# Stream weights one place later, a gate product that waits, and a decay by TensorE and ScalarE, in a fused mLSTM and latent attention step

## The reference, cut to what matters

```python
s = jnp.einsum('bhtd,bhsd->bhts', q, k) * w_intra
num = w_inter[..., None] * jnp.einsum('bhvk,bhtk->bhtv', C, q) + jnp.einsum('bhts,bhsv->bhtv', s, v)
...
decay = jnp.exp(b_last + m - m_new)
C_new = decay[..., None, None] * C + jnp.einsum('bhsv,bhsk->bhvk', v * w_upd[..., None], k)
n_new = decay[..., None] * n + jnp.einsum('bhs,bhsk->bhk', w_upd, k)
...
y = (hn.astype(x.dtype) + skip * xc) * jax.nn.silu(z)
```

## Time and profile before

| | |
|---|---|
| median of 3 runs | 992.86 us (992.49 to 997.19) |
| profiled execution | 993.93 us, its span 992.0 us |
| PE busy | 970.4 us (98% of the span) |
| DVE busy | 558.6 us (56%) |
| POOL busy | 480.8 us (48%) |
| ACT busy | 413.8 us (42%) |
| HBM traffic over the span | 165 GB/s in the mean, 330 to 416 GB/s in the slices of the heads |

### The profile page before, as it was taken

One profiled execution on the slowest core, in us unless ns is written; L12 is line 12 of the kernel. 1 busy time (PEld: TensorE's weight loads), 2 busy tenths in 40 slices (PEclk: granted clock), 3 DMA queues, 4 the chain that ended last, 5 costly groups with the idle time before them and its releaser, 6 DMA issues.

```text
span 992.0 us, 11792 instructions
## 1 busy us (share of the span) xinstructions
PE 970.4 (98%) x4220; PEld 622.8 (63%) x4220; DVE 558.6 (56%) x1126; ACT 413.8 (42%) x810; POOL 480.8 (48%) x434
## 2 busy tenths in 40 slices
PE   7999999999989999999999999999999999999998
PEld 5776776767645353443535777777766666657885
DVE  5875572745667677976856522246734444456445
ACT  3576876766674734537231000011222423243221
POOL 1585885977525847668364262233630303133330
PEclk9999999999989999999999999999999999999999
DMA  7215134343286998999898422203210111203202
GB/s 281 91 60 211 61 111 162 112 147 127 85 332 230 376 416 330 394 370 361 336 341 334 154 85 85 84 23 109 97 66 32 57 43 45 110 16 134 87 24 106
DMA packets 45721, 164.37 MB, mean 166 GB/s; under 512 B 4884, under 2 KB 8344, under 8 KB 36704
## 3 DMA queue, kind: packets, MB, share of 16 engines
q1 hardware_dynamic: 45664, 163.63, 44.7%
HBM read 106.33 MB, written 57.28 MB: 165 GB/s over the span
## 4 chain that ended last, share of the span: by engine, by line
PE 66%; DVE 4%; ACT 1%; issue 1%; DMA 0%; SPq 0%; ACTq 0%; DVEq 0%
PE work_a L1188 5%; PE bank L1314 5%; PE work_b L1611 5%; PE work_a L834 4%; PE work_a L1164 4%; PE work_b L1485 3%; PE bank L1155 3%; PE work_b L834 3%; PE work_b L1140 3%; PE work_b L1314 3%; PE bank L1572 2%; PE work_a L1597 2%; PE bank L1206 2%; PE work_a L1557 1%; PE work_b L1473 1%; PE bank L1731 1%
## 5 line engine op out<-in xcount | busy, mean ns | idle before, releaser
L3057 POOL TENSOR_TENSOR arena<-arena 128x640 f32<-128x640 f32 x96 | 138.7, 1462 | 36.7 <-ACT arena L1772 34.2
L2560 DVE SCALAR_TENSOR_TENSOR arena<-arena,bank 128x512 f32<-128x512 f32 x128 | 87.0, 742 | 38.1 <-PE bank L1155 38.1
L3260 POOL COPY arena<-arena 32x640 f32<-32x640 f32 x20 | 19.2, 959 | 121.3 <-ACT arena L2097 115.0
L956 PE MATMUL work_a<-arena,ring 128*128 128x320 f32 x224 | 64.9, 433 | 0.0
L956 PE MATMUL work_a<-arena 128*128 128x320 f32 x224 | 64.9, 433 | 0.0
L956 PE MATMUL work_b<-arena 128*128 128x320 f32 x224 | 62.7, 433 | 0.0
L1188 PE MATMUL work_a<-arena 128*128 128x512 f32 x128 | 61.2, 606 | 0.0
L956 PEld LDWEIGHTS work_b<-arena 128*128 128x128 f32 x224 | 42.7, 191 | 17.6
L956 PEld LDWEIGHTS work_a<-arena 128*128 128x128 f32 x224 | 42.7, 190 | 17.6
L956 PEld LDWEIGHTS work_a<-arena,ring 128*128 128x128 f32 x224 | 42.4, 190 | 17.2
L1826 ACT ACTIVATE bank<-arena 128x320 f32<-128x320 f32 x96 | 47.0, 522 | 3.5
(11 more groups left out here) (432 smaller groups left out, 2144.7 us busy)
## 6 DMA issues: line engine op xcount, KB each, us to landing
ring<-in_stream SPq DMA_DIRECT2D x66, 512.0 KB, 3.4
arena<-in_c SPq DMA_DIRECT2D x32, 1024.0 KB, 8.1
out_s_c<-arena SPq DMA_DIRECT2D x32, 1024.0 KB, 5.9
arena<-in_keys SPq DMA_DIRECT2D x8, 664.0 KB, 4.1
z_scratch<-arena SPq DMA_DIRECT2D x16, 320.0 KB, 3.1
v_scratch<-arena SPq DMA_DIRECT2D x20, 256.0 KB, 2.3
k_scratch<-arena SPq DMA_DIRECT2D x4, 1280.0 KB, 5.3
arena<-k_scratch SPq DMA_DIRECT2D x4, 1280.0 KB, 9.3
```

The source lines that it names most:

```text
L956: last = mm(quarter[q], weights[:, k, :], tokens_of[:, k, :], start=fresh and k == 0, stop=k == KH - 1, skip_group_check=True)
L2560: op = v.scalar_tensor_tensor(ct[s % CS][:, g, :], ct[s % CS][:, g, :], decb[:, h, b:b + 1], bank[g][:, :], ALU.mult, ALU.add)
L3057: op = g.tensor_tensor(dst, dst, parts[(adds[0] - adds[1]) % len(parts)], ALU.add)
```

## The change

It has three parts.

`stream_weights(h + 1)` leaves the place ahead of `weight_args(h + 1)` and stands behind `weighted_scores(h + 1, 1)`, for each of the 3 changes of head. Its wait on `m_rows` goes to `weight_args`. Head 0's own instance ahead of the loop stays.

POOL's `gated(h, prompt)` gets one more wait in heads 0 to 2: for all 5 of `weight_args(h + 1)`.

`first_n` goes. In its place `decsel` is made 4 times as wide (4x128, once for each q), a second matmul with one output column turns it into a decay for each of the 128 rows, DVE's copy takes that column along (33 columns for 32), and ACT multiplies `n_rows` by it, in head 0 between `normalise(0, 3)` and `next_keys(0, 0)`. The host sends `p_rows` as zeros, so the load L702 has 260 columns for 164. The wait of `new_n(0)` is now on ACT's instruction.

```diff
-        decsel = shaped(kwsum[:, 0, 0:HEADS * STREAMS], (HEADS, STREAMS))
-        decb = take(HEADS, STREAMS)
+        decsel = shaped(kwsum[:, 0, 0:KH * GROUP], (KH, HEADS, STREAMS))
+        decb_rows = take(GROUP + 1)
+        decb, dec_rows = shaped(decb_rows[:, 0:GROUP], (HEADS, STREAMS)), decb_rows[:, GROUP:GROUP + 1]
...
-            op = mm(bank[0][:, DEC_AT:DEC_AT + HEADS * STREAMS], ones_f[0:HEADS, :],
-                                decsel[0:HEADS].rearrange("p a b -> p (a b)"), start=True, stop=True)
+            mm(bank[0][:, DEC_AT:DEC_AT + GROUP], ones_f[0:HEADS, :], decsel[0:HEADS, 0].rearrange("p a b -> p (a b)"),
+               start=True, stop=True)
+            op = mm(bank[0][:, DEC_AT + GROUP:DEC_AT + GROUP + 1], decsel[0:HEADS].rearrange("p q a b -> p (q a b)"),
+                    ones_f[0:HEADS, 0:1], start=True, stop=True)
...
                 normalise(h, 3)
+                if h == 0:
+                    act.wait_ge(base_in, 16 * 4)
+                    nc.scalar.activation(n_rows, n_rows, ACT.Copy, scale=dec_rows).then_inc(n_decayed, 1)
                 next_keys(h, 0)
...
             def stream_weights(h):
-                if h:
-                    dve.wait_ge(m_rows, 16 * (h + 2))
...
             def weight_args(h):
                 if h:
+                    dve.wait_ge(m_rows, 16 * (h + 2))
...
-            def first_n():
-                dve.wait_ge(base_in, 16 * 4)
-                selected = p_rows[:, 0:GROUP]
-                op = v.tensor_tensor(selected, decb.rearrange("p a b -> p (a b)"), own_dec, ALU.mult)
-                op.then_inc(dve_own, c.up(dve_own))
-                dve.wait_ge(dve_own, c.all(dve_own))
-                v.reduce_sum(dec_rows, selected, AX_X).then_inc(dve_own, c.up(dve_own))
-                dve.wait_ge(dve_own, c.all(dve_own))
-                v.tensor_scalar(n_rows, n_rows, dec_rows, None, ALU.mult).then_inc(dve_own, c.up(dve_own))
-                v.memset(p_rows, 0.0).then_inc(dve_own, c.up(dve_own))
-                dve.wait_ge(dve_own, c.all(dve_own))
...
                 if h == 0:
-                    first_n()
+                    dve.wait_ge(n_decayed, N_DECAYED)
...
-                    head_front(h + 1)
+                    weight_args(h + 1)
...
                     weighted_scores(h + 1, 1)
+                    stream_weights(h + 1)
                     stream_queries(h + 1)
...
+                if more:
+                    pool.wait_ge(dmax_ready, TT * (h + 2))
                 gated(h, slice(0, SEQ), 1)
```

More of the change, by code:

```diff
@@ L270, in program @@
          pv_mm, norm_done, turn_mm, turn_out, pc_mm, pc_out, y_added, weights_summed, prod_mm, prod_kept, prod_sum, y_mixed, pool_mixed, basis_x_ready, inverse_in_sbuf, inverse_in_psum) = (sem(n) for n in names)
+        n_decayed, N_DECAYED = inverse_in_psum, 2
         x_in = [sem(f"x_in{n}") for n in range(4)]
@@ L367, in program @@
         assert top[0] <= c_at, top[0]
[L369 to L372, removed]
+        n_input = rstd[:, HALF:HALF + 2 * P + HEADS]
+        both_rows, p_rows, n_rows = (n_input[:, a:b] for a, b in ((0, 2 * P), (0, P), (P, 2 * P)))
+        own_row = n_input[:, 2 * P:2 * P + HEADS]
         gate_rows, b_row, a2 = arena[:, 0:HALF], rstd[:], msel
@@ L2465, in _ @@
             onehot = rowc[R, R_ONEH:R_ONEH + HEADS]
-            op = v.tensor_tensor(decsel[R], dec_row[R, 0:STREAMS].unsqueeze(1).to_broadcast([HEADS, HEADS, STREAMS]),
-                                            onehot.unsqueeze(2).to_broadcast([HEADS, HEADS, STREAMS]), ALU.mult)
+            op = v.tensor_tensor(decsel[R], dec_row[R, 0:STREAMS].unsqueeze(1).unsqueeze(1).to_broadcast([HEADS, KH, HEADS, STREAMS]),
+                                            onehot.unsqueeze(1).unsqueeze(3).to_broadcast([HEADS, KH, HEADS, STREAMS]), ALU.mult)
             op.then_inc(sel_ready, c.up(sel_ready))
             dve.wait_ge(G.bfill[0], c.next(G.bfill[0]))
-            op = v.tensor_copy(decb.rearrange("p a b -> p (a b)"), bank[0][:, DEC_AT:DEC_AT + HEADS * STREAMS])
+            op = v.tensor_copy(decb_rows, bank[0][:, DEC_AT:DEC_AT + GROUP + 1])
             op.then_inc(cols_ready, c.up(cols_ready))
@@ L2590, in add_skip @@
                                            h_t[:, q, part], ALU.mult, ALU.add).then_inc(raised, c.up(raised))
-            def head_front(h):
-                stream_weights(h)
-                weight_args(h)
             dve.wait_ge(bc_out, 1)
@@ L3456, in _lay_out @@
     n0 = at("state_mlstm_n")[0][..., within].reshape(STREAMS, HEADS, KH, P).transpose(3, 1, 2, 0)
-    row = np.arange(P) % GROUP
-    n_rows = np.concatenate([n0.transpose(2, 1, 3, 0).reshape(P, P), row[:, None] // STREAMS == np.arange(HEADS)[None, :],
-                             row[:, None] == np.arange(GROUP)[None, :]], axis=1).astype(f)
+    row_head = np.arange(P) % GROUP // STREAMS
+    n_rows = np.concatenate([np.zeros((P, P), f), n0.transpose(2, 1, 3, 0).reshape(P, P),
+                             row_head[:, None] == np.arange(HEADS)[None, :]], axis=1).astype(f)
     half = ROPE // 2
```

## The result

| | before | changed |
|---|---|---|
| median, 7 runs each, side by side | 995.75 us | 989.09 us |
| ratio changed / before | | 0.9942 (95%: 0.9923 to 0.9962) |
| profiled execution: time, span | 993.93, 992.0 us | 990.84, 988.9 us |

The ratio is 5.8 us, between 3.8 and 7.7.

A forecast was written before the change was run, and what follows sets the result against it. PE, busy 98%, was taken as the bound, so only its waits and slow spells pay. Back 3.87 + 2 x 1.20 = 6.27, lost 0.3 + 3 x 0.2 = 0.9: 5.4 us less, 987.5 us, range 986.4 to 990.6.

The forecast's parts named there:

- `first_n` off DVE: Change from head 0 to 1: PE's 2.4 us wait and the clock dip behind it go, 3.87 us back.
- next in line: Head 0 to 1, what could hold PE next: POOL's sums (2.8 us spare), step 7's C tile (0.4), DVE's list (2.9).
- The decay on ACT: Head 0: one ACT instruction of 0.4 us, load wait 0 to 0.3, swallowed by idle time; PE loses nothing.
- The wider selection and the second matmul: Ahead of the heads, on PE's path: 0.2 us for the matmul and 0.1 for the selection, 0.3 lost once.
- The stream weights moved, the product held: Later two changes of head: first weighted scores begin 1.4 us earlier, 1.20 us back each; 0.2 lost per change.
- The term of 0.2 us: Each of three changes of head: loss from the queue behind `stream_weights` and a collision with POOL, ends 0 and 0.55.
- The product later: POOL's gate product ends 2 us later; `inverse_root` and the next load of z behind it lose nothing.
- The wait in `weight_args`: Head 0: the wait for the prompt's C store, reached 4 us earlier, may hold DVE where it waits for PE anyway.
- The moved collision: Rival: POOL's small instructions and sum hit the stream work, up to 1.2 us per head change; 990.5 us, chance 0.18.
- The clock-or-DMA case: Rival, head 0: a late C tile or clock dip leaves only 1.8 of 3.87 us back; 989.6 us, chance 0.13.
- The slower one: Rival, head 0: ACT waits for the `n_rows` load, deciding at about 15 us landing; 995.5 us, chance 0.03.
- The signs: Right: PE's waits gone, clock 1.00, head changes 16.5 to 17 us. Wrong: C-tile wait, over 0.6 us lost ahead of heads.

The follow-up runs named there:

- e1: Kernel before with the stream weights moved and the gate product held, `first_n` left on DVE: ratio 0.9988 to the kernel before.
- e2: Changed kernel with both moves undone, leaving only the decay by a matmul and ACT: ratio 0.9980 to the kernel before.
- e3: Changed kernel without POOL's new wait, so the gate product is not held: ratio 0.9985 to the kernel before.
- e4: Changed kernel with `stream_weights` back ahead of the weight arguments and POOL's wait kept: ratio 0.9932 to the kernel before.
- e5: Changed kernel with the stream queries one place later, behind tile 2's weighted scores: ratio 0.9953 to the kernel before.
- e9: Changed kernel with the load of `n_rows` issued one step later: ratio 1.0036 to the kernel before, span 995.5 us.
- e8: Changed kernel, unedited, run again on another chip with a second profile: ratio 0.9956 to the kernel before, span 987.9 us.

## Why the prediction was right, point by point

**The time.** Forecast 987.5 us from a median of 992.86, 0.54% less, in a range of 986.4 to 990.6. Measured were 989.09 and ratios of 0.58% and 0.44% less. The later runs showed that 992.86 was a low median for the kernel before (others 993.4 to 995.75), so the ratio is the better measure, and 5.4 us lies inside both its intervals (3.8 to 7.7 and 2.9 to 5.8). That the medians came so near is partly luck. The spans of the two profiles are only 3.1 and 4.1 us shorter: the heads gave 4.3 and 5.0 us, where the forecast had 5.7, and 1.3 and 1.2 were lost ahead of them, where it had 0.3.

**What bounds it.** Right: PE's two waits were `first_n` (e1, e2) and the gate product (e3, e4), each shown by itself.

**`first_n` off DVE, 3.87 us.** The wait and the dip are gone, as said. The term was too large by the wait for the C tile: A of head 0 came to 6.85 and 6.08, not 5.93. That was the second of the "next in line", with 0.4 us to spare by the prediction. It became a wait of 0.85 us, because the tile landed 12.7 us behind its issue, not 11.4; issue and need had both moved by the same 1.3 us. The rival had this at a cost of 2 us with the dip; it came at 0.9 at most, and without one.

**The decay on ACT: nothing.** Right. The instruction took 0.42 us, and ACT still sat idle 0.69 us ahead of its transposes, where it had 0.98. Its wait for the load was 0 (0.79 in e5, without a wait of PE).

**The wider selection and the second matmul, 0.3 us.** Right by themselves: the matmul costs 0.2 (S is 7.52 in e1, 7.72 to 7.74 in seven others), and the selection took 0.28 us for 0.18. What the step didn't see is that this place is bound by a DMA landing too, so that what PE gains upstream can be lost there. The trace of the kernel before had it, as DVE's selection began 2.4 us behind the instruction ahead of it:

```profile
297.16 0.18 DVE L2466 TENSOR_TENSOR arena<-arena 4x32 f32<-4x32 f32 x1 [2.38 <-issue]
```

**The stream weights moved, the product held, 1.20 less 0.2 each.** Measured by B: 0.84, and by the period 0.93. The term of 0.2 us was the mis-sized one: it is 0.36. The cause given for most of it was wrong too. I counted the queue behind the stream weights as a tie, with a loss of 0 to 0.2, and added a collision with POOL's small instructions. The stream weights took 0.415 us in all instances, so there was no collision that held them; the loss is the tie, which went against PE by 0.36. POOL was what stretched: its last small instruction took 1.25 us beside the queries, 0.27 without them.

**The product later.** It cost nothing, as said.

**The wait in `weight_args`** for the prompt's C did hold DVE, for 1.86 us in head 0, ahead of step 7's updates, and PE didn't notice it, as said.

**The rivals.** The moved collision did not occur. The clock-or-DMA case did by its cause, at under half its price. The slower one has its price shown in e9, and it was priced too low: a landing at about 334, 16 us behind the issue of 318.5, was enough for +0.36%, 3.6 us, where the text had +2.6 us for 18. What it left out is the dip, 2.4 us beside PE's wait of 5.1. So the point of decision must lie nearer than the 15 us of the text; no run shows where.

**The signs.** Most of those for "right" came: the waits are gone, the clock stood at 1.00, the later changes of head took 16.82 us. The change of head 0 to 1 took 17.74 in the first profile, outside the 16.5 to 17 (16.97 in e8). And two of those for "wrong" came as well, the wait for a C tile and a loss of over 0.6 us ahead of the heads (1.3 and 1.2).

The Trainium skill's rule ("SBUF — State Buffer", section "Who interferes with whom"), that the DVE instruction with two SBUF inputs is blocked until a GpSimd instruction that reads SBUF and started first has ended, is borne out by e3 for a second kind of instruction: 3.93 us for 0.34, ended 0.15 us behind the product. For POOL's one-element instructions the trace doesn't show it: L2500 started at 419.34 inside one (from 419.04, 0.55 us; POOL's spans are rough) and still took 0.41 us.

## What to carry to other kernels

When an instruction beside a long one of another engine takes ten times its usual time, moving it can just hand the delay to the next of its kind, as here. Hold the long one until the short ones are through, and check that nobody waits for it (e3 against e4). Measure a fix by the period of the loop and not by the stretch that it was meant for, since a wait can step out of the stretch (e5). And when a wait goes, list what lands or ends next behind it: here a C tile with 0.4 us to spare, and a store ahead of the loop whose landing bounds what can be won before it.

## What the runs showed of the hardware beyond what was expected

In the heads, PE's waits of 2.4 us (before, e1) and 5.1 us (e9) went with a spell at 1.2 GHz: the granted clock was 0.50 from 351 to 353 us before, behind the wait that ended at 349.6, and from 338 to 342 in e9, where it fell while PE still waited. Waits of 0.2 to 0.9 us in the heads of the changed kernel, e2, e3, e4 and e5 were not followed by one (1.00 from 345 to 545 us). Ahead of the heads a spell followed even a wait of 0.2 us, behind a row of matmuls with 4 rows (before: 0.50 from 300 to 302 us). The spell of before in head 0 cost about 1.5 us (3.87 - 2.38) beside a wait of 2.4.
